# Where the moving rows and the joined rows begin in on-chip memory: start bytes of three operand tiles of a two-part transformer

## The chip, the cores and the metric

The kernel runs on one core of one Trainium2 chip. The metric is the device time of that core in microseconds, as the median of three runs. Four engines matter: TensorE (PE, its weight loads listed apart as PEld), VectorE (DVE), ScalarE (ACT) and, little used here, GpSimd (POOL). SyncE issues the weight transfers.

## What is computed

The reference takes x of 256 rows and 1024 columns through two blocks of two layers each, all in float32.

```python
# first block, layer l
h = rms_norm(x, g_mix[l]); proj = h @ w_in[l]
y_a, y_b, y_c, y_d = ...        # top-k attention, long convolution, short convolution, stick-breaking attention
merged = g0*y_a + g1*y_b + g2*y_c + g3*y_d
x = x + merged @ w_merge[l]
h2 = rms_norm(x, g_ffn[l]); gt = causal_dwconv(h2 @ w_ffn_gate[l], ffn_conv_w[l])
x = x + (silu(gt) * (h2 @ w_ffn_up[l])) @ w_ffn_down[l]
# second block, layer l
x = x + attention(rmsnorm(x, norm_mix[l])) @ w_out     # compressed attention in layer 0, dilated attention in layer 1
a, b = split(rmsnorm(x, norm_ffn[l]) @ w_up); x = x + (silu(a) * b) @ w_down
```

## The kernel before, in words

**The weights** come as a stream of 277 units of 1 MB (`weight_units`), each 1024 x 256, 256 x 1024 or 512 x 512. SyncE loads unit n into one of three slots of `raw`; ACT copies it, rounded, into one of four slots of `whi` (`make_high`, L439); DVE, for some units POOL, writes the remainder raw - whi into one of three slots of `wlo` (`make_low`, L447). A slot is used again when PE is through with the unit that was in it. Activations are split the same way into a high and a low half.

**Every large product** then consists of three matmuls for each pair of operand blocks (`three_passes`, L471 to L473): high by high, high by low, low by high. Each has a stationary block of 128 columns (512 bytes in each partition) that is loaded before the matmul, and a moving block of 256 columns (1024 bytes) or 512 columns (2048 bytes).

```python
nc.tensor.matmul(dst, left[0], right[0], start=first, stop=False)
nc.tensor.matmul(dst, left[0], right[1], start=False, stop=False)
return nc.tensor.matmul(dst, left[1], right[0], start=False, stop=last)
```

**The stages** run one after the other: a mixer or attention stage, an output product (`add_rows_product`), the up stage of the feed-forward (`ffn_up_stage`), its down product (again `add_rows_product`), and so on for four layers.

- `add_rows_product` (from L792) multiplies `joined` (the merged rows, or the context of an attention: 4 units, 96 matmuls) or `hidden` (the feed-forward's inner rows, `fT`: 11 units, 264 matmuls) with a weight unit. `joined` or `hidden` is stationary, the weights move, 512 columns at a time. At its end PE transposes the new x (L555), and ACT and DVE write the high and the low half of it, multiplied by the gain but not yet by the row's norm, to a tile of unscaled rows: `mixer_rows`, `ffn_rows`, `blocks_rows` or `dilated_rows`, after the stage that follows (`raw_T`, L542).
- A mixer or an up stage starts on these unscaled rows, so that PE need not wait for the norm. Unit 0 goes through `first_unit` (L656, L657, L665), then PE spreads the norm over the partitions (L597), then units 1 to 3 use the unscaled rows through `three_passes`. Meanwhile DVE and ACT write the scaled rows `hT`, and unit 4 and all later ones use `hT`. The weights are stationary here and the rows move, 256 columns at a time, but for units 4 to 11, 22 and 23 of a mixer and the first units of the attention stages, where the rows are stationary and the weights move.
- In an up stage (22 units, 48 matmuls each), DVE does for each pair of units the gate's part, the low half of the inner rows and two `make_low`, in an order written out by hand (`ffn_up_stage`, the vector engine's loop). Unit 5 needs the `make_low` that DVE does after the second pair's gate.

**Where tiles begin** is fixed by the order of allocation and, for tiles laid over a larger one, by a start in float32 elements (`over`, L269). The first tile, x, begins at byte 2176 of a partition. The starts that matter, modulo 512:

| tile | start given in the code | byte modulo 512 |
|---|---|---|
| `whi`, `wlo`, every slot | own tiles, 51840 and 84608 | 128 |
| `hT` | h_place (byte 10368) + 112 elements | 64 |
| `joined` | h_place + 96 elements | 0 |
| `hidden` | work (byte 120384) + 16 elements | 128 |
| `mixer_rows`, `ffn_rows` | work + 19072, + 14464 elements | 64 |
| `dilated_rows`, `query_rows`, `branch` | work + 17920, + 13824, + 4096 elements | 64 |
| `blocks_rows` | work + 15456 elements | 448 |

All blocks within a tile are multiples of 512 bytes apart, so an operand has its tile's start.

```python
hT_both = over("hT", at_h, LEAD_ROWS, [2, KT, S])                  # LEAD_ROWS = 512 // 4 - 16 = 112
joined_both = over("joined", at_h, LEAD_ROWS - 16, [2, KT, S])
for kind, rows_at in (("mixer", 19072), ("ffn", 14464), ("blocks", 15456), ("dilated", 17920)):
    raw_T[kind] = [over(f"{kind}_rows{i}", at_work, rows_at + i * KT * S, [KT, S]) for i in range(2)]
```

Of the kernel before, what the change touches and what calls it, by code (L numbers as in the profile page):

```python
# [30 lines left out]
S = 256  # L31
TT = S // P
KT = D // P
# [200 lines left out]
def two_part_transformer(nc, a, consts, onehots, out):  # L234
    ctx = ExitStack()
    with ctx:
# [11 lines left out]
        LEAD_ROWS = PHASE - 16  # L248
# [18 lines left out]
        at_h, at_work = place["h_place"], place["work"]  # L267

        def over(name, base, start, shape, dt=F32R):  # L269

            return nc.alloc_sbuf_tensor_at(name, [P] + shape, dt, offset=base + 4 * start)

        hT_both = over("hT", at_h, LEAD_ROWS, [2, KT, S])
        hT = [hT_both[:, i] for i in range(2)]
        joined_both = over("joined", at_h, LEAD_ROWS - 16, [2, KT, S])
        joined = [joined_both[:, i] for i in range(2)]

        ROWS = 32
# [261 lines left out]
            root_ready.close(n)  # L540

        raw_T = {}  # L542
        for kind, rows_at in (("mixer", 19072), ("ffn", 14464), ("blocks", 15456), ("dilated", 17920)):
            raw_T[kind] = [over(f"{kind}_rows{i}", at_work, rows_at + i * KT * S, [KT, S]) for i in range(2)]
        part_sum = stat[:, 152:156]
        root = stat[:, 4:4 + TT]
# [2266 lines left out]
```

How the kernel before makes its waits and increments, by code:

```python
        def begin(eng):  # L397
            if stage[0]:
                eng.wait_ge(stage_done.sem, COMPUTE * stage[0])
# [1 line left out]
        def end(eng):  # L401
            eng.drain().then_inc(stage_done.sem, 1)
# [10 lines left out]
        def v_wait(n):  # L413
            nc.vector.wait_ge(vector_step.sem, n)
# [9 lines left out]
        def s_wait(n):  # L424
            nc.scalar.wait_ge(scalar_step.sem, n)
# [6 lines left out]
        def make_high(act, upto):  # L432
            while stream.high < min(upto, len(stream.units)):
                n = stream.high
                act.wait_ge(raw_landed[n % RAW_SLOTS], 16 * (n // RAW_SLOTS + 1))
                if n >= HIGH_SLOTS:
                    act.wait_ge(*stream.freed[n - HIGH_SLOTS])
                act.activation(part(whi, n, HIGH_SLOTS), part(raw, n, RAW_SLOTS), ACT.Copy).then_inc(high_made, 1)
                stream.high += 1
# [1 line left out]
        def make_low(eng, n):  # L442
            eng.wait_ge(high_made, n + 1)
            if n >= LOW_SLOTS:
                eng.wait_ge(*stream.freed[n - LOW_SLOTS])
            eng.tensor_tensor(part(wlo, n, LOW_SLOTS), part(raw, n, RAW_SLOTS),
                              part(whi, n, HIGH_SLOTS).bitcast(F32), ALU.subtract).then_inc(stream.low[n][0], 1)
# [10 lines left out]
        def take_unit(pe, n):  # L459
            pe.wait_ge(*stream.low[n])
            _, kt, _, _ = stream.units[n]
            return [part(b, n, k).rearrange("p (k c) -> p k c", k=kt) for b, k in ((whi, HIGH_SLOTS), (wlo, LOW_SLOTS))]
# [18 lines left out]
        def await_pair(pe):  # L482
            if handed_over:
                pe.wait_ge(*handed_over.pop(0))
```

## Time and profile before

| | |
|---|---|
| median of 3 runs | 1798.43 us (1796.06 to 1802.86) |
| the profiled execution | 1797.66 us, of it 1795.9 us from the first to the last instruction |
| mean granted TensorE clock | 0.983 of full speed |
| PE | 1738.4 us busy, 13416 matmuls |
| DVE, ACT, POOL | 1226.3, 932.3, 125.0 us busy |
| memory traffic | 305.75 MB, mean 170 GB/s |

PE busy merges the times of matmuls that overlap, so a stage in which they follow each other without a gap counts as wholly busy, however far apart they start. What tells how fast PE works is the spacing: the time from the start of one matmul to the start of the next. A matmul's own duration (0.28 us at 256 columns, 0.39 us at 512) is over twice the spacing.

### The profile page before, as it was taken

How to read it: one execution, taken by the hardware profiler on the slowest of the kernel's cores; microseconds unless marked ns; L12 is line 12 of the kernel's file. 1: busy time of each engine (PE TensorE's matmuls, PEld its weight loads, DVE VectorE, ACT ScalarE, POOL GpSimd, SP SyncE). 2: the span in 40 equal slices, each digit the busy share in tenths (PEclk: the TensorE clock that was granted, in tenths of full speed). 3: DMA queues.
4: the chain of work that ended last, by engine and by line, in shares of the span. 5: the costliest groups of instructions: out<-in, count | busy, mean ns of one | idle time of the engine just before them, and what ended most of it. 6: DMA issues, size and time to landing. Idle time of an engine off the chain costs nothing.

```text
span 1795.9 us, 31735 instructions
## 1 busy us (share of the span) xinstructions
PE 1738.4 (97%) x13416; PEld 1641.0 (91%) x13416; DVE 1226.3 (68%) x1927; ACT 932.3 (52%) x1291; POOL 125.0 (7%) x35
## 2 busy tenths in 40 slices
PE   6999999999999999999999998889999999999998
PEld 6989999899989999999999898769998999889986
DVE  6994956797649868467887475977554656666553
ACT  5446655454445546654644356756443655655432
POOL 1620300000004503000000000000000000000000
PEclk9899999999999999999999989989999999999999
DMA  7684546556554554546465555415555486436551
GB/s 232 183 204 132 188 135 207 165 176 197 192 198 156 182 168 126 187 158 217 142 201 185 184 160 146 142 48 164 192 185 200 166 213 160 130 119 210 188 199 70
DMA packets 248636, 305.75 MB, mean 170 GB/s; under 512 B 9266, under 2 KB 223630, under 8 KB 248495
## 3 DMA queue, kind: packets, MB, share of 16 engines
q1 hardware_dynamic: 235959, 289.66, 49.3%
q10 hardware_dynamic: 12536, 14.06, 4.2%
q8 instruction: 106, 1.74, 0.4%
q14 instruction: 35, 0.29, 0.0%
HBM read 299.51 MB, written 4.19 MB: 169 GB/s over the span
## 4 chain that ended last, share of the span: by engine, by line
PE 76%; DVE 15%; ACT 4%; DMA 3%; issue 2%; DVEq 0%; ACTq 0%; SPq 0%
PE psum L471 23%; PE psum L472 22%; PE psum L473 22%; DVE wlo L447 3%; DVE psum L1482 3%; DMA raw<-in_w_in 1%; DVE work L1614 1%; PE psum L2483 1%; PE psum L2509 1%; DVE work L1612 1%; DMA raw<-in_a_w_in 1%; PE psum L2495 1%; ACT whi L439 1%; DMA raw<-in_b_w_q 1%; DVE work L1628 1%
## 5 line engine op out<-in xcount | busy, mean ns | idle before, releaser
L439 ACT ACTIVATE whi<-raw 128x2048 fp32r<-128x2048 f32 (+2 forms) x277 | 525.1, 1901 | 370.8 <-PE psum L473 261.3
L447 DVE TENSOR_TENSOR wlo<-raw,whi 128x2048 fp32r<-128x2048 f32 x249 | 566.8, 2281 | 198.0 <-PE psum L473 164.4
L471 PE MATMUL psum<-hT,whi 128*128 128x256 f32 x2160 | 608.2, 282 | 2.9 <-DVE wlo L447 1.5
L472 PE MATMUL psum<-hT,whi 128*128 128x256 f32 x2160 | 604.8, 280 | 0.0
L473 PE MATMUL psum<-hT,wlo 128*128 128x256 f32 x2160 | 604.7, 280 | 0.0
L471 PEld LDWEIGHTS psum<-hT,whi 128*128 128x128 f32 x2160 | 410.8, 190 | 4.2 <-DVE wlo L447 2.2
L472 PEld LDWEIGHTS psum<-hT,whi 128*128 128x128 f32 x2160 | 407.4, 189 | 0.2
L473 PEld LDWEIGHTS psum<-hT,wlo 128*128 128x128 f32 x2160 | 407.4, 189 | 0.0
L447 POOL TENSOR_TENSOR wlo<-raw,whi 128x2048 fp32r<-128x2048 f32 (+1 forms) x28 | 123.8, 4423 | 575.5 <-ACT whi L439 396.0
L471 PE MATMUL psum<-whi,hidden 128*128 128x512 f32 x352 | 137.2, 390 | 1.0 <-issue 1.0
L473 PE MATMUL psum<-whi,hidden 128*128 128x512 f32 x352 | 137.0, 389 | 0.0
L472 PE MATMUL psum<-wlo,hidden 128*128 128x512 f32 x352 | 137.0, 389 | 0.0
L1482 DVE SCALAR_TENSOR_TENSOR psum<-work,par,psum 128x256 f32<-128x256 f32 x240 | 94.6, 481 | 0.1
L471 PE MATMUL psum<-whi,hT 128*128 128x256 f32 (+1 forms) x320 | 92.4, 289 | 0.0
L472 PE MATMUL psum<-wlo,hT 128*128 128x256 f32 (+1 forms) x320 | 92.1, 288 | 0.0
L473 PE MATMUL psum<-whi,hT 128*128 128x256 f32 (+1 forms) x320 | 91.8, 287 | 0.0
L471 PEld LDWEIGHTS psum<-whi,hidden 128*128 128x128 f32 x352 | 66.1, 188 | 15.4 <-issue 1.7
L473 PEld LDWEIGHTS psum<-whi,hidden 128*128 128x128 f32 x352 | 66.1, 188 | 13.8
L472 PEld LDWEIGHTS psum<-wlo,hidden 128*128 128x128 f32 x352 | 66.1, 188 | 13.5
L910 ACT ACTIVATE work<-work 128x512 f32<-128x512 f32 x22 | 13.9, 633 | 118.6 <-DVEq L958 118.6
L1250 ACT ACTIVATE work<-psum 128x512 f32<-128x512 f32 (+1 forms) x40 | 23.2, 580 | 94.1 <-PE psum L473 94.0
L471 PE MATMUL psum<-branch,whi 128*128 128x256 f32 x256 | 71.3, 279 | 0.0
(367 smaller groups left out, 3073.1 us busy)
## 6 DMA issues: line engine op xcount, KB each, us to landing
raw<-in_w_in SPq DMA_DIRECT2D x78, 1024.0 KB, 5.5
raw<-in_ffn_w_up SPq DMA_DIRECT2D x44, 1024.0 KB, 5.0
raw<-in_w_ffn_gate SPq DMA_DIRECT2D x22, 1024.0 KB, 5.1
raw<-in_w_ffn_up SPq DMA_DIRECT2D x22, 1024.0 KB, 5.2
raw<-in_w_ffn_down SPq DMA_DIRECT2D x22, 1024.0 KB, 4.8
raw<-in_ffn_w_down SPq DMA_DIRECT2D x22, 1024.0 KB, 4.9
raw<-in_b_w_q SPq DMA_DIRECT2D x12, 1024.0 KB, 6.0
raw<-in_a_w_in SPq DMA_DIRECT2D x10, 1024.0 KB, 5.1
```

The costliest lines, as they stand in the source:

```text
L439: act.activation(part(whi, n, HIGH_SLOTS), part(raw, n, RAW_SLOTS), ACT.Copy).then_inc(high_made, 1)
L447: eng.tensor_tensor(part(wlo, n, LOW_SLOTS), part(raw, n, RAW_SLOTS), part(whi, n, HIGH_SLOTS).bitcast(F32), ALU.subtract).then_inc(stream ...
L471: nc.tensor.matmul(dst, left[0], right[0], start=first, stop=False)
L472: nc.tensor.matmul(dst, left[0], right[1], start=False, stop=False)
L473: return nc.tensor.matmul(dst, left[1], right[0], start=False, stop=last)
L1250: ins = act.activation(views[0], src[:, :, 0:views[0].shape[-1]], func)
L1482: ins = dve.scalar_tensor_tensor(acc, glu[:, ct, k:k + S], tap, acc, ALU.mult, ALU.add)
L1612: ins = dve.tensor_scalar(score[:, t, 0:L], rel[t][:, h, :], w, None, ALU.mult)
L1614: ins = dve.scalar_tensor_tensor(score[:, t, 0:L], rel[t][:, h, :], w, score[:, t, 0:L], ALU.mult, ALU.add)
L1628: n[t] = v_done(dve.match_replace(score[:, t, 0:L], top[:, t, :], score[:, t, 0:L], TAKEN))
L2483: mm = nc.tensor.matmul(slot(e)[:, st * keys:(st + 1) * keys], d_q[j // 2 % 2][lo:lo + DH, st, j % 2, t * P:(t + 1) * P], d_k[lo:lo + DH, ...
L2495: mm = nc.tensor.transpose(turn_bank(s, m)[:, i * P:(i + 1) * P], probs[:, 2 * (s % 2) + e, n * P:(n + 1) * P], ident)
```

## The change

`joined` begins at element 0 of its place in place of element 96, and the unscaled rows of the mixers and of the feed-forward stages 16 elements (64 bytes) later. By the table above, all three then begin at byte 128 modulo 512. No instruction is added, removed or moved in the program's order.

```diff
@@ -272,7 +272,7 @@
         hT_both = over("hT", at_h, LEAD_ROWS, [2, KT, S])
         hT = [hT_both[:, i] for i in range(2)]
-        joined_both = over("joined", at_h, LEAD_ROWS - 16, [2, KT, S])
+        joined_both = over("joined", at_h, 0, [2, KT, S])
         joined = [joined_both[:, i] for i in range(2)]
@@ -540,7 +540,7 @@
         raw_T = {}
-        for kind, rows_at in (("mixer", 19072), ("ffn", 14464), ("blocks", 15456), ("dilated", 17920)):
+        for kind, rows_at in (("mixer", 19088), ("ffn", 14480), ("blocks", 15456), ("dilated", 17920)):
             raw_T[kind] = [over(f"{kind}_rows{i}", at_work, rows_at + i * KT * S, [KT, S]) for i in range(2)]
```

## Rows read from the trace of the kernel before

**Rows 1.** The page: busy time of each engine, and its share of the chain.
```profile
PE 1738.4 (97%) x13416; PEld 1641.0 (91%) x13416; DVE 1226.3 (68%) x1927; ACT 932.3 (52%) x1291; POOL 125.0 (7%) x35
...
PE 76%; DVE 15%; ACT 4%; DMA 3%; issue 2%; DVEq 0%; ACTq 0%; SPq 0%
```
**Rows 2.** PE timeline (start us, us), first product of `joined`: first matmul, and what follows the last.
```profile
329.22 0.47 PE L471 MATMUL psum<-whi,joined 128*128 128x512 f32 x1 [0.26 <-issue]
...
351.60 0.60 PE L555 MATMUL psum<-cst,x 128*128 128x128 f32 x4
```
**Rows 3.** PE timeline, first product of `hidden`: first matmul, and what follows the last.
```profile
478.72 0.47 PE L471 MATMUL psum<-whi,hidden 128*128 128x512 f32 x1 [0.26 <-issue]
...
538.67 0.49 PE L555 MATMUL psum<-cst,x 128*128 128x128 f32 x3
```
**Rows 4.** PE timeline, first up stage: unit 1's second matmul, unit 4's first.
```profile
360.18 0.28 PE L472 MATMUL psum<-ffn_rows,whi 128*128 128x256 f32 x1
...
376.39 0.28 PE L471 MATMUL psum<-hT,whi 128*128 128x256 f32 x1
```
**Rows 5.** PE timeline, second up stage: the same two matmuls.
```profile
865.74 0.28 PE L472 MATMUL psum<-ffn_rows,whi 128*128 128x256 f32 x1
...
882.58 0.28 PE L471 MATMUL psum<-hT,whi 128*128 128x256 f32 x1
```
**Rows 6.** Windows, PE: window, its us, busy (matmuls), PEclk, DMA share, GB/s; rows moving.
```profile
354.30:359.30 5.00, 5.00 (x45) 1.00 0.01 3
549.00:563.00 14.00, 14.00 (x121) 1.00 0.36 100
...
1610.00:1624.00 14.00, 14.00 (x121) 1.00 0.49 156
```
**Rows 7.** The same view: `hT` moving, up stages 1, 2 and 4, then one mixer stretch.
```profile
384.00:476.00 92.00, 92.00 (x784) 1.00 0.61 204
884.00:984.00 100.00, 100.00 (x852) 1.00 0.60 198
...
1627.00:1711.00 84.00, 84.00 (x716) 1.00 0.59 197
791.40:834.30 42.90, 42.90 (x381) 1.00 0.55 196
```
**Rows 8.** The same view: before and after three changes of operands without a stop.
```profile
65.00:94.00 29.00, 29.00 (x249) 1.00 0.88 204
95.60:111.20 15.60, 15.60 (x140) 1.00 0.91 219
...
674.00:684.00 10.00, 10.00 (x91) 1.00 0.04 11
685.00:705.00 20.00, 20.00 (x172) 1.00 0.79 252
1061.00:1068.00 7.00, 7.00 (x64) 1.00 0.47 150
1069.00:1079.00 10.00, 10.00 (x88) 1.00 1.00 239
```
**Rows 9.** DVE timeline: the low half of unit 5, first three up stages.
```profile
379.74 2.29 DVE L447 TENSOR_TENSOR wlo<-raw,whi 128x2048 fp32r<-128x2048 f32 x1
...
885.57 2.29 DVE L447 TENSOR_TENSOR wlo<-raw,whi 128x2048 fp32r<-128x2048 f32 x1
...
1249.91 2.29 DVE L447 TENSOR_TENSOR wlo<-raw,whi 128x2048 fp32r<-128x2048 f32 x1
```
**Rows 10.** PE timeline: unit 5 begins, first stage (at 382.08) and second (888.23).
```profile
381.71 0.28 PE L473 MATMUL psum<-hT,wlo 128*128 128x256 f32 x1
382.08 0.39 PE L471 MATMUL psum<-hT,whi 128*128 128x256 f32 x1
382.31 0.28 PE L472 MATMUL psum<-hT,whi 128*128 128x256 f32 x1
...
888.23 0.28 PE L471 MATMUL psum<-hT,whi 128*128 128x256 f32 x1
```

## The prediction

> **What bounds the kernel now.** I read the page first. PE is busy 97% of the span, most slices show a 9, the granted clock is near full nearly everywhere, and the chain that ended last runs through PE for 76% [rows 1]. The change moves no instruction, so it can act only through how fast an engine reads or writes the moved tiles. PE is the engine to look at, and its busy time is of no use for this: overlapping matmuls count as busy whatever their spacing. So I went on to the timeline and took spacings, as the time between two starts over the number of matmuls between them. In the windows view a matmul counts when any part of it falls in the window, so there the spacing is (width + 0.28 us) / count.
>
> At 512 moving columns, `joined` takes 351.60 - 329.22 = 22.38 us for 96 matmuls, 233.1 ns each [rows 2]. `hidden` takes 538.67 - 478.72 = 59.95 us for 264, 227.1 ns each [rows 3]. Shape, line and moving tile are the same, both stages have a stall-free run, and what differs is the stationary tile's start: byte 0 modulo 512 for `joined`, 128 (that of the weights) for `hidden`. That is the best evidence that starts matter.
>
> At 256 columns there are two speeds. Units 1 to 3 of the first up stage: (376.39 - 360.18) / 143 = 113.4 ns [rows 4]. The same units of the second: (882.58 - 865.74) / 143 = 117.8 ns [rows 5]. Same tiles, same starts (rows at 64, weights at 128), other speed. So an unequal start doesn't set the speed but allows two, 4.4 ns apart. The slow one holds in units 1 to 3 of three up stages and of the second mixer and in unit 0 of the first up stage: 14.28 / 121 = 118.0 ns at 549, 117.0 and 118.0 at the last two up stages (one matmul of count is 1 ns there), 5.28 / 45 = 117.3 in unit 0 [rows 6]. `hT`, also at 64, runs at 92.28 / 784 = 117.7 ns through four up stages, yet at 43.18 / 381 = 113.3 ns in a mixer [rows 7]. A speed, once taken, lasts for hundreds of matmuls, until PE stops or the operands change.
>
> **The change part by part.** *`joined` to 128.* Afterwards it has exactly the starts of `hidden`, so I price it at its spacing: 4 products x 96 x (233.1 - 227.1) ns = 2.3 us, all on PE's path, since the stage before and after waits for it. Bounds: 0 if the difference had another cause, 2.3 if not.
>
> *The rows to 128.* No row shows 256 moving columns at equal starts. The bounds are 113.4 ns (the fast speed) and, on the bad side, half of the largest single spacing in the `joined` product, some 120.5 ns as an estimate (rows 2 give its mean, 116.5 per 256 columns, which is the nearer figure of that row). I take 113.4, because the only equal-start row, `hidden`, is 113.5 per 256 columns [rows 3] and keeps it through its whole run. Then:
> - Units 1 to 3 of up stages 3 and 4 and of mixer 2: 143 x 4.4 ns = 0.63 us each, 1.9 us. In up stage 3 the low half of unit 5 ends at 1249.91 + 2.29 = 1252.2 [rows 9], and PE gets to unit 5 only some 5 us later, so nothing takes it back; stage 4 is the same program.
> - Up stage 2: PE would be 0.63 us earlier, but DVE ends the low half of unit 5 at 885.57 + 2.29 = 887.86 [rows 9] and PE now begins it at 888.23 [rows 10]. Only 0.37 us of lead is there, and a stop costs a restart: the first spacing after one is 382.31 - 382.08 = 0.23 us instead of 0.12 in stage 1 (its first matmul lasts 0.39 instead of 0.28 us) [rows 10]. I keep 0.2 us. What is late next is DVE, which has the gate, the convolution and the low half in front of it.
> - Up stage 1: already fast in units 1 to 3, and it shows this stop: PE waits from 381.71 + 0.11 to 382.08, DVE having ended at 379.74 + 2.29 = 382.03 [rows 9, 10]. Only unit 0 gains, 47 x 4.4 ns = 0.2 us; DVE's chain begins with the norm behind unit 0 and moves with it.
>
> *Writes of the moved tiles* by ACT and DVE: same instructions, starts still multiples of 64 bytes. Nothing for them; `joined` is last written just before its product, so a dearer write would show there, and it would have to be 8 writes of each half, against which no row speaks and for which none does.
>
> Sum: 2.3 + 1.9 + 0.2 + 0.2 = 4.6 us. From the profiled execution's 1797.66 us that gives **1793.1 us**. The median of the runs is 0.8 us above that execution; the spread of the three, 6.8 us, is larger than the sum.
>
> **The large unknown: what `hT` does after the rows.** It runs 18 units of 48 matmuls in each up stage, 864 x 4.4 ns = 3.8 us if its speed flips. Today stages 2 to 4 go from slow rows to slow `hT` and stage 1 from fast to fast, until its stop, after which `hT` is slow (rows 4, 5 and 7 together). With the change the moving start goes from 128 to 64 at that point. Three changes of operands without a stop show a moving start going from 128 to 64: at 95.5 slow (29.28 / 249 = 117.6) turns fast (15.88 / 140 = 113.4), at 684 fast (10.28 / 91 = 113.0) turns slow (20.28 / 172 = 117.9), at 1068 fast (7.28 / 64 = 113.8) turns slow (10.28 / 88 = 116.8) [rows 8]. Each turned into the other. By that, fast rows hand a slow `hT`, as now, and the 3.8 us per stage stay where they are. I choose that.
>
> **The rivals.** *`hT` inherits the fast speed* where no stop follows, up stages 3 and 4: 2 x 3.8 = 7.7 us more, **1785.4 us**. For it: fast rows went to fast `hT` in stage 1, without a stop. Against: there the start did not change, and the three changes of [rows 8].
>
> *Only `joined` gains*: 256 columns settle in the slow speed at equal starts too, where stage 1 then loses what it has. **About 1795.4 us**, 1797.66 - 2.3.
>
> *Starts don't matter at all*, and `joined` is slow for another reason, such as its short run: **1797.7 us**. For it, two speeds at equal addresses; against it, two products that differ in one thing only. The Trainium skill, page "TensorE: Matmul & The Clock Gate", section "Step-by-step: what each phase is for", gives PE one read port for the moving operand and one for weight loads and says that loading the next weights takes no bandwidth from the running matmul; by it the change would be worth nothing, and this rival would be the forecast. The difference of rows 2 and 3 doesn't follow from it.
>
> *Equal starts collide at 256 columns.* The load of the next weights (512 bytes) and the moving rows (1024 bytes) begin at the same byte of the 512, and at 256 columns the next load begins as the last ends, which at 512 columns it doesn't. Place: the 6 x 192 = 1152 matmuls on moved rows, of which 4 x 143 + 47 are slow now, mean 115.8 ns. At 120.5 ns: 1152 x 4.7 ns = 5.4 us, less 2.3 for `joined`: **1800.8 us**. It decides against the change from 115.8 + 2.0 = 117.8 ns on, the present slow speed, and passes the 0.5% bound at about 126 ns. For it: no row of such a product. Against: `hidden`.
>
> **How the numbers follow.** Forecast 0.52; `hT` fast 0.18; only `joined` 0.12; nothing 0.06; collision 0.12. A measurement of this kernel can tell about 0.5%, 9 us, from no change, so faster means below 1789.4. The `hT` rival gives 0.17 of that; the forecast 0.07, where up stages 1 and 2 restart fast as well (2 x 3.8 us) or stops elsewhere fall on the fast side: faster 0.24. Slower: half the collision, and 0.03 for restarts that fall slow and for the clock, 0.09. Same 0.67. The range reaches down to the `hT` rival and up to the collision's price, 1785 to 1800.5; the forecast's own range is 1789 to 1797.
>
> **What would show it.** The `joined` product at about 227 ns and 21.8 us; units 1 to 3 of all up stages and mixer 2 at 113.4; `hT` behind them at 117.8 in stages 3 and 4, and a stop before unit 5 in stage 2. Rows at over 117.8 ns, or `joined` still at 233, would prove the sum wrong; `hT` at 113.3 over a whole up stage would prove the choice at the handover wrong.

## The result, and the profile after

The changed kernel takes 1786.88 us (median of 6 runs, 1785.55 to 1792.08) against 1798.51 us before (6 runs, 1796.06 to 1802.86): a ratio of 0.9939, 95% interval 0.9922 to 0.9956. That is 11.6 us less, inside the range of the prediction, but two and a half times the 4.6 us of its sum, and it came in another way: two large terms that the sum did not hold, of opposite sign, left a time within the range, which is in part luck. The profiled execution has a span of 1784.1 us, against 1795.9.

The page of the changed kernel, busy times and chain's engine:

```profile
PE 1725.9 (97%) x13416; PEld 1630.3 (91%) x13416; DVE 1226.8 (69%) x1927; ACT 931.5 (52%) x1291; POOL 125.1 (7%) x35
```

Against [rows 1] the counts are the same and DVE and ACT are as busy as before; PE is busy 12.5 us less, which is the whole gain. Nothing was hidden and nothing moved: the same matmuls follow each other more closely.

The PE timeline of the changed kernel (start us, us), in the order of [rows 2], [rows 4] and [rows 5]: the first `joined` product, then unit 1's second matmul and unit 4's first in up stages 1 and 2:

```profile
330.82 0.47 PE L471 MATMUL psum<-whi,joined 128*128 128x512 f32 x1 [0.27 <-issue]
...
352.69 0.38 PE L555 MATMUL psum<-cst,x 128*128 128x128 f32 x2
...
361.37 0.28 PE L472 MATMUL psum<-ffn_rows,whi 128*128 128x256 f32 x1
...
378.53 0.28 PE L471 MATMUL psum<-hT,whi 128*128 128x256 f32 x1
...
865.39 0.28 PE L472 MATMUL psum<-ffn_rows,whi 128*128 128x256 f32 x1
...
882.55 0.28 PE L471 MATMUL psum<-hT,whi 128*128 128x256 f32 x1
```

`joined` takes 21.87 us for 96 matmuls instead of 22.38: 0.51 us in each of four products, 2.0 us. The moved rows take (378.53 - 361.37) / 143 = 120.0 ns a matmul, and the same in stage 2, where 113.4 and 117.8 ns stood before. They became slower than either speed of before.

The windows of the changed kernel (window, its us, busy and matmuls, granted clock, DMA share, GB/s): first the rows in up stage 1, in the mixer and in up stage 4, as in [rows 6]; then `hT` moving in up stages 1, 2 and 4, as in [rows 7]; the third is like the fourth in both:

```profile
362.00:376.00 14.00, 14.00 (x119) 1.00 0.47 148
547.00:561.00 14.00, 14.00 (x119) 1.00 0.37 99
...
1600.00:1614.00 14.00, 14.00 (x119) 1.00 0.47 151
385.00:475.00 90.00, 90.00 (x797) 1.00 0.64 210
888.00:980.00 92.00, 92.00 (x814) 1.00 0.63 207
...
1624.00:1714.00 90.00, 90.00 (x797) 1.00 0.59 195
```

Rows: 14.28 / 119 = 120.0 ns in each. `hT`: 90.28 / 797 = 113.3 ns in all four up stages, against 117.7 in [rows 7]. So the gain is in `hT`, whose place did not change. How one passes to the other, up stage 1 (PE timeline; the first row is the last matmul on the rows):

```profile
378.41 0.28 PE L473 MATMUL psum<-ffn_rows,wlo 128*128 128x256 f32 x1
378.53 0.28 PE L471 MATMUL psum<-hT,whi 128*128 128x256 f32 x1
...
379.12 0.28 PE L473 MATMUL psum<-hT,wlo 128*128 128x256 f32 x1
...
476.36 0.28 PE L473 MATMUL psum<-hT,wlo 128*128 128x256 f32 x1
```

The first five spacings take 0.59 us, 118 ns each, and the 858 behind them (476.36 - 379.12) / 858 = 113.3 ns each, without a stop. At unit 5 there is none either: DVE ends its low half at 380.83 + 2.29 = 383.12, and PE, held up by the slower rows, comes only at 384.0.

```profile
380.83 2.29 DVE L447 TENSOR_TENSOR wlo<-raw,whi 128x2048 fp32r<-128x2048 f32 x1
```

**The sum by parts.** `joined` -2.0 us. `hT` in the up stages -15.4 us: in stage 1 from the first `hT` matmul to the first of the down product 476.89 - 378.53 = 98.36 us instead of 478.72 - 376.39 = 102.33, and 864 x 4.4 ns = 3.8 in each other. The rows +4.7 us, as an estimate: stage 1 17.16 - 16.21 = 0.95; stages 2 to 4 and mixer 2, 143 x 2.2 ns = 0.3 each; some 0.8 in mixer 1; 48 x 6 ns = 0.3 in each of the five units 0 that were fast. Together -12.7; the span shrank by 11.8, and the 0.9 us left are in the mixers and attentions, whose stretches change speed from execution to execution.

### The profile page after: what moved, and what is told of

It is laid out like the page before. It is cut to its first block, busy times and chain, and to the rows that moved or that the text cites. A ratio compares the mean times of both kernels' runs of the same rounds, so it can differ in the third digit from the quotient of the medians.

```text
span 1784.1 us, 31735 instructions
## 1 busy us (share of the span) xinstructions
PE 1725.9 (97%) x13416; PEld 1630.3 (91%) x13416; DVE 1226.8 (69%) x1927; ACT 931.5 (52%) x1291; POOL 125.1 (7%) x35
## 4 chain that ended last, share of the span: by engine, by line
PE 77%; DVE 14%; ACT 4%; DMA 4%; issue 2%; DVEq 0%; SPq 0%; ACTq 0%
PE psum L471 23%; PE psum L473 23%; PE psum L472 23%; DVE wlo L447 3%; DVE psum L1482 3%; DVE work L1614 1%; DMA raw<-in_w_in 1%; PE psum L2483 1%; ACT whi L439 1%; PE psum L2509 1%; DMA raw<-in_a_w_in 1%; PE psum L2495 1%; DMA raw<-in_b_w_q 1%; PE psum L656 1%; DVE work L1628 1%
```

## The experiments

The theory: **a moving block of 256 columns that begins where the weights do costs 120.0 ns. From 64 bytes before, two speeds are possible, 113.3 and 117.8 ns, and which one it is stays until PE stops or the operands change. What is handed over from a run at 120.0 ns is always the fast one.** The last sentence is put to the test below, and holds for less than it says. The rivals are named with each group of runs. "Draw" is short for a speed that neither the starts nor the instructions of a stretch fix; what does fix it was not found. Each run's profile is one execution; its times are of 4 to 10 runs, beside runs of the kernel before on the same chip.

### One part alone, and `hT` at equal starts

```diff
-        joined_both = over("joined", at_h, LEAD_ROWS - 16, [2, KT, S])
+        joined_both = over("joined", at_h, 0, [2, KT, S])
```


> Only joined at byte 128, all rows still at 64. Handover theory (the rows at 128 run at 120.0 ns and it is their handing over to hT that makes hT fast): joined products 226.7 ns a matmul, 2.3 us gained, units 1 to 3 of the up stages and hT behind them as before (117.8 ns in the four up stages), about 1796 us. Rival (the draw of hT's speed hangs on anything earlier, such as joined's own timing): hT fast in some up stages, each worth 3.8 us, 1781 to 1792 us.

```diff
-        ... ("mixer", 19072), ("ffn", 14464) ...
+        ... ("mixer", 19072), ("ffn", 14480) ...
```


> Only the feed-forward's unscaled rows at byte 128. Handover theory: 768 matmuls on these rows at 120.0 ns, some 2.9 us lost against the mean of before, and 863 matmuls on hT in each of four up stages at 113.3 ns, 15.3 us gained; no stop of PE before unit 5; sum about 1786 us. Rival (joined's start had a part in it): hT slow, 117.8 ns, in some or all of the four stages, 1790 to 1801 us.

```diff
-        ... ("mixer", 19072), ("ffn", 14464) ...
+        ... ("mixer", 19088), ("ffn", 14464) ...
```


> Only the mixers' unscaled rows at byte 128. Both theories: these 384 matmuls at 120.0 ns, 1 to 2 us lost, the matmuls on hT behind them not faster as a whole, since in a mixer the next units have hT stationary and stops for the transposes follow every few units; 1798 to 1801 us. Handover theory: the up stages as before. If the handover worked in the mixers too, the 47 matmuls of unit 4 would be at 113.3 ns in both.

On the changed kernel:
```diff
-        hT_both = over("hT", at_h, LEAD_ROWS, [2, KT, S])
+        hT_both = over("hT", at_h, 0, [2, KT, S])
```


> The changed kernel with hT at byte 128 as well. If equal starts of the weights and of a moving block of 256 columns cost 120.0 ns whatever comes before: all 6480 matmuls with hT moving at 120.0 ns. Of the changed kernel 5026 of them were at 113.3 and about 1400 at 117.8: 33 + 3 us lost, about 1822 us. Rival (120.0 ns belongs to the rows' place in the stage and not to their start): hT at 113.3 to 117.8 ns, 1780 to 1800 us.

| kernel | median us (runs) | ratio to before, 95% interval |
|---|---|---|
| `joined` alone | 1796.31 (10) | 0.9974, 0.9954 to 0.9994 |
| feed-forward rows alone | 1786.82 (4) | 0.9924, 0.9910 to 0.9939 |
| mixers' rows alone | 1801.36 (10) | 0.9995, 0.9977 to 1.0013 |
| all, and `hT` at 128 too | 1813.11 (4) | 1.0069, 1.0054 to 1.0084 |

The feed-forward's rows, 16 elements further on, carry the change: alone they give what the whole gives. `hT` in the four up stages, windows as above, of the kernel with the feed-forward's rows alone:

```profile
386.00:476.00 90.00, 90.00 (x797) 1.00 0.63 204
...
1627.00:1717.00 90.00, 90.00 (x797) 1.00 0.61 199
```

of the kernel with `joined` alone:

```profile
385.00:475.00 90.00, 90.00 (x796) 1.00 0.65 208
885.00:975.00 90.00, 90.00 (x766) 1.00 0.62 198
...
1628.00:1718.00 90.00, 90.00 (x767) 1.00 0.58 189
```

and of the kernel with the mixers' rows alone (its stage 2 is as slow as its stage 1):

```profile
386.00:476.00 90.00, 90.00 (x767) 1.00 0.62 197
...
1264.00:1354.00 90.00, 90.00 (x796) 1.00 0.61 201
1635.00:1725.00 90.00, 90.00 (x767) 1.00 0.58 188
```

797 matmuls in 90 us are 113.3 ns, 766 are 117.9. With the feed-forward's rows at 128, four of four are fast. With them at 64, one of four is fast, and not the same one: stage 1 in one kernel, behind its stop before unit 5, stage 3 in the other. Before the change none was. Neither kernel changed anything in these stages, so at unequal starts the speed of a stage is a draw. It is not an even one in every place: the 191 matmuls on `hT` at 283.68 us of the kernel before are slow in all seven kernels that have `hT` in one piece at 64 there. I had written for `joined` alone that the up stages would be as before; for stage 1 that missed, and the rival there, that any earlier timing plays a part, has this much right.

For the mixers' rows I had asked for one thing more: by the handover, unit 4, which has `hT` as the stationary side, should be fast in both mixers. It was in the first and not in the second, and the changed kernel does the same. There, without a stop behind rows at 120.0 ns (PE timeline of the changed kernel, mixer 1 and mixer 2; the last line is the first matmul of the next unit):

```profile
42.18 0.28 PE L472 MATMUL psum<-wlo,hT 128*128 128x256 f32 x1
...
47.39 0.28 PE L473 MATMUL psum<-whi,hT 128*128 128x256 f32 x1
...
562.70 0.28 PE L471 MATMUL psum<-whi,hT 128*128 128x256 f32 x1
...
568.36 0.19 PE L471 MATMUL psum<-whi,hT 128*128 128x68 f32 x1
```

That is (47.39 - 42.18) / 46 = 113.3 ns and (568.36 - 562.70) / 48 = 117.9 ns. So "always the fast one" fails where the operands change sides. Where the moving side alone passes from a costly start to 64 or 320 it holds in every trace: in all sixteen up stages of four kernels (the changed one, the feed-forward's rows alone, the two with `hT` at 320 and with stops, below), and for `branch` at 64 behind `hT` at 128 or 0, eight times in eight.

`hT` at 128 gives 752 in 90 us, 90.28 / 752 = 120.1 ns, in a stage where nothing else was touched: 120.0 ns belongs to the equal start, and not to the rows' part of the stage.

```profile
900.00:990.00 90.00, 90.00 (x752) 1.00 0.61 194
66.00:95.00 29.00, 29.00 (x244) 1.00 0.89 201
308.00:329.00 21.00, 21.00 (x188) 1.00 0.47 167
```

The second window has `hT` as the stationary side in mixer 1 and the weights moving: 29.28 / 244 = 120.0 ns, where `hT` at 64 gives 117.6 [rows 8]. So it is the two starts together that cost, and not a moving start of 128 by itself. The third is `branch`, at 64, behind `hT` at 128: 21.28 / 188 = 113.2 ns.

The time was forecast at 1822 us and is 1813. The up stages pay in full (3456 x 6.7 ns = 23 us). In the mixers the `branch` products were fast, and part of the slower matmuls may fall where PE would have waited for DVE, which no run took apart.

### A map of the starts

On the changed kernel, `joined` left at 128:
```diff
-  hT at h_place + 112, mixer_rows at 19088, ffn_rows at 14480
+  hT at h_place +  96, mixer_rows at 19056, ffn_rows at 14496
```


> A map of starts, joined at 128 throughout; the weights stay at 128. Here hT and the mixers' rows at 0, the feed-forward's rows at 192. Theory 'two speeds at any unequal start': these rows at 113.3 or 117.8 ns, hT at one of the two for a whole up stage as the draw falls, 1780 to 1796 us. Rival 'a start 128 bytes off collides' (joined at 0 took 233.1 ns at 512 columns): hT above 117.8 ns, over 1800 us.

```diff
+  hT at h_place +  16, mixer_rows at 19024, ffn_rows at 14528
```


> hT at 192, the mixers' rows at 384, the feed-forward's rows at 320. Theory of two speeds: 113.3 or 117.8 ns on all three, 1780 to 1796 us. Rival 'only a start after the weights' is free of the slow speed, since only starts before them were tried with rows moving': hT at 113.3 ns everywhere, about 1777 us.

```diff
+  hT at h_place +  80, mixer_rows at 18992, ffn_rows at 14560
```


> hT and the feed-forward's rows at 448, the mixers' rows at 256. Theory of two speeds: 113.3 or 117.8 ns on all three, 1780 to 1796 us. Rival 'distance decides': at 192 bytes from the weights no slow speed, hT at 113.3 ns in all four up stages and in the mixers, about 1772 us (rows fast too).

```diff
+  hT at h_place +  48, mixer_rows at 18976, ffn_rows at 14576
```


> hT at 320, the mixers' rows at 192, the feed-forward's rows at 0. Theory of two speeds: 113.3 or 117.8 ns on all three, 1780 to 1796 us. Rival 'distance decides': hT at 113.3 ns in all four up stages and the mixers, about 1772 us.

They took 1804.94, 1803.59, 1803.52 and 1784.85 us (ratios 1.0026, 1.0015, 1.0020 and 0.9917, the last with an interval of 0.9890 to 0.9945). In windows of the first: `hT` at 0, mixer rows at 0.

```profile
895.00:985.00 90.00, 90.00 (x761) 1.00 0.62 200
551.00:565.00 14.00, 14.00 (x119) 1.00 0.37 97
```

Of the second: `hT` at 192, mixer rows at 384, and, last, `hT` stationary in a mixer.

```profile
898.00:988.00 90.00, 90.00 (x766) 1.00 0.63 202
34.00:42.00 8.00, 8.00 (x69) 1.00 0.55 163
592.00:614.00 22.00, 22.00 (x197) 1.00 0.53 156
```

Of the fourth: the feed-forward's rows at 0, `hT` at 320 behind them, the rows again in stage 3, and `hT` in mixer 1.

```profile
362.00:376.00 14.00, 14.00 (x119) 1.00 0.44 142
889.00:979.00 90.00, 90.00 (x797) 1.00 0.66 210
1230.00:1245.00 15.00, 15.00 (x129) 1.00 0.50 161
181.00:201.00 20.00, 20.00 (x172) 1.00 0.75 234
```

The rows at 0 take 15.28 / 129 = 118.4 ns in stage 3, where stage 1 has 120.0. `hT` at 320 takes 20.28 / 172 = 117.9 ns in the mixer and 113.3 in the up stage.

| moving start modulo 512, weights at 128 | ns a matmul of 256 columns |
|---|---|
| 128, 384 | 120.0 |
| 0, 256 | 118.7 or 120.0 (both seen at 0) |
| 64, 320 | 113.3 or 117.8 |
| 192, 448 | 113.3 or 117.8, behind a stop nearly always 117.8 |

Starts 256 bytes apart behave alike, so what seems to count is the start modulo 256; the weights stood at 128 throughout. The last two rows differ: of the stretches of 40 or more matmuls with `hT` moving behind a stop, 110 of 197 were slow at 64 or 320, and 44 of 46 at 192 or 448 (PE timelines of ten kernels). Both rivals fell: a start further off (448) or one after the weights (192) is not better, since `hT` at 192 and 448 had the slow speed in all eight up stages, and in the fourth kernel `hT` was fast in the up stages but not throughout the mixers. The rival that a start 128 bytes off costs more than 117.8 ns held, for 0 and 256. I had expected two speeds there, and under 1796 us for the first three.

The fourth kernel supports the handover. Its rows are at 0, a costly start but another one, and `hT` at 320, which no kernel had tried: four of four up stages at 113.3 ns. That 320 is fast by itself, the rival here, is ruled out by the slow window in its mixer. And where `hT` is the stationary side and the weights move, a start at 192 or 448 was fast nearly throughout (22.28 / 197 = 113.1 ns), where 64 is mostly slow [rows 8].

### How few matmuls set the speed, and what a stop does

On the changed kernel the rows go back to 64 modulo 256, but for the last of their eight blocks:
```diff
+        class Halved:
+            def __init__(self, name, base, start):
+                self.body = over(name, base, start, [KT - 1, S])
+                self.tail = over(name + "_tail", base, start + (KT - 1) * S + 16, [1, S])
+            def __getitem__(self, at):
+                p, k, c = at
+                return self.tail[p, 0, c] if k == KT - 1 else self.body[p, k, c]
...
+            raw_T[kind] = [Halved(f"{kind}_rows{i}", at_work, rows_at - 64 + i * (KT * S + 64)) ...    # 19072, 14464
```


> The changed kernel with the mixers' and feed-forward's unscaled rows at byte 64 modulo 256 again, but for the last of their eight blocks of 256 columns, which alone begins at 128. Handover theory (a few matmuls at 120.0 ns are enough to set the fast speed for what follows): hT fast, 113.3 ns, in all four up stages, and the rows at 113.3 ns for most of the 21 matmuls behind each three slow ones, mean 114.5 to 115.5 instead of 120.0: 5 to 6 us less than the changed kernel, about 1781 us. Rival (the whole run of rows at 120.0 is needed, or what counts is that PE arrives late at unit 5): hT at 117.8 ns in at least two of the up stages, 1788 to 1796 us.

The same, and for `hT`:
```diff
+        hT = [Halved(f"hT{i}", at_h, 48 + i * (KT * S + 64)) for i in range(2)]
```


> The same, with the last block of hT at 128 as well (the rest of hT at 64 modulo 256). Handover theory: every group of 24 matmuls has three at about 120 ns and some transition, the rest at 113.3 whatever the stops did: mean about 115 ns for hT moving. Against the kernel of the run before this one, the up stages lose some 3456 x 1.5 ns = 5 us, and the mixers and attentions gain on the 1400 matmuls that are slow now, 1400 x 2.8 ns = 4 us: about the same, 1778 to 1785 us. Rival (the fast speed after a few matmuls is not kept): mean above 116.5 ns, over 1790 us.

On the changed kernel, in the up stage's PE loop:
```diff
                     w = take_unit(pe, n0 + n)
+                    if n in (6, 14):
+                        pe.drain()
```


> The changed kernel, with PE drained ahead of units 6 and 14 of each up stage. A stop costs at most 0.5 us, 8 of them 2 to 4 us. Theory (a stop draws the speed anew, the handover's gain lasts until then): hT fast in units 4 and 5 of each up stage, then fast or slow for stretches of 8 units (384 matmuls, 1.7 us each), some of the 8 slow: 1788 to 1800 us. Rival (hT's speed belongs to the addresses now in use, stops or not): all stretches at 113.3 ns, 1788 to 1791 us.

`hT` in the up stages in one piece as in the first of these, in halves as in the second in the mixers and the compressed attention:


> The kernel with the last block of the rows at 128 (median 1779.97 us), with hT in one piece at 64 in the up stages, and with its last block at 128 in the mixers and in the compressed attention alone. Theory: the up stages keep 113.3 ns, in the mixers hT moving goes from a mix of 113.3 and 117.8 to a mean of about 115, and branch behind it is fast; against the run with the last block at 128 everywhere 3456 x 1.0 = 3 to 5 us less, about 1777 us. Rival (the kept state is lost at every stop for the transposes, so that the slow matmuls cost as much as they save there): 1780 us or more.

| kernel | median us (runs) | ratio to before, 95% interval |
|---|---|---|
| last block of the rows | 1779.97 (4) | 0.9898, 0.9862 to 0.9935 |
| last block of rows and `hT` | 1781.44 (4) | 0.9911, 0.9879 to 0.9942 |
| two stops in each up stage | 1797.16 (10) | 0.9988, 0.9971 to 1.0005 |
| last block of the rows, and of `hT` in the mixers | 1782.28 (6) | 0.9904, 0.9879 to 0.9928 |

**The stops** gave back most of the gain, 10.3 us by medians of different sessions, 9 by the two ratios. Each costs some 0.4 us (in stage 1, 392.24 to 392.84 us for what takes 0.23 otherwise), 3 us in all; three slow stretches of 382 matmuls are 5 us. The profiled execution is 14.5 us longer than that of the changed kernel: 8.2 us in the four up stages, as this sum says, and 6.4 in the mixers and attentions, where nothing was changed. Windows of that kernel, the two stretches behind the stops in stages 1, 2 and 3:

```profile
394.00:436.00 42.00, 42.00 (x359) 1.00 0.65 206
440.00:482.00 42.00, 42.00 (x359) 1.00 0.61 200
904.00:944.00 40.00, 40.00 (x342) 1.00 0.66 207
950.00:990.00 40.00, 40.00 (x356) 1.00 0.62 210
1272.00:1312.00 40.00, 40.00 (x356) 1.00 0.58 190
1317.00:1357.00 40.00, 40.00 (x355) 1.00 0.56 185
```

Units 4 and 5 ahead of the first stop were fast in all four stages. Behind it: slow, slow, slow, fast, fast, fast (42.28 / 359 = 117.8, 40.28 / 342 = 117.8, 40.28 / 356 = 113.1), and fast twice in stage 4. Same instructions, same addresses: behind a stop the speed is a draw again.

**Three matmuls** in 24 are enough for the rest. One turn of the loop in the kernel with the rows' last block at 128, PE timeline:

```profile
363.34 0.28 PE L480 MATMUL psum<-ffn_rows_tail,whi 128*128 128x256 f32 x1
363.46 0.27 PE L481 MATMUL psum<-ffn_rows_tail,whi 128*128 128x256 f32 x1
363.57 0.28 PE L482 MATMUL psum<-ffn_rows_tail,wlo 128*128 128x256 f32 x1
363.69 0.28 PE L480 MATMUL psum<-ffn_rows,whi 128*128 128x256 f32 x1
```

The spacings around the tail are 0.11 to 0.12 us, and then 0.113 on average until the next tail. Its windows, the rows in stage 1 and `hT` in stages 2 and 4:

```profile
362.00:376.00 14.00, 14.00 (x125) 1.00 0.47 151
890.00:980.00 90.00, 90.00 (x797) 1.00 0.64 210
1625.00:1715.00 90.00, 90.00 (x796) 1.00 0.61 199
```

The rows take 14.28 / 125 = 114.2 ns instead of 120.0, and `hT` is fast in all four stages. 1152 x 5.8 ns would be 6.7 us, and the medians are 6.9 us apart. That agreement is loose: the medians are of different sessions, the intervals of the two ratios overlap, and the profiled execution, the slowest of the four, is 2.6 us shorter in the up stages and 3.8 longer in the rest. By its median the kernel is the fastest of the study. In stages 1 and 2 the stop before unit 5 is back, and the draw with it: in this profile it fell fast twice, in that of the last kernel it fell slow in stage 1:

```profile
384.00:474.00 90.00, 90.00 (x766) 1.00 0.63 205
```

With `hT`'s last block at 128 too, the up stages run at 90.28 / 791 = 114.1 ns with no draw left in them, and the mixers' `branch` products were fast; what that gains it pays in the up stages. The last kernel was to have both, 1777 us, and took 1782.28 us, the time of its rival. The rival's reason does not hold, though. Windows of it, `hT` moving behind a stop and then `hT` stationary, in the mixers:

```profile
287.00:307.00 20.00, 20.00 (x177) 1.00 0.60 214
580.00:609.00 29.00, 29.00 (x247) 1.00 0.61 182
```

With `hT` moving the expected mean came, 20.28 / 177 = 114.6 ns, stops or not. With `hT` stationary the block at 128 costs and hands nothing on: 29.28 / 247 = 118.5 ns, above both speeds of before. That and the slow stage 1 cost time; how the 5 us split was not measured. The medians of the three, 1780.0 to 1782.3 us, are nearer to each other than their intervals are wide.

## Why the prediction was right and wrong

- **`joined` to 128: right.** 2.3 us forecast, 2.0 us in the profile. Alone it measures 0.26%, 0.06 to 0.46%, which is 4.7 us and holds 2.3; draws of the up stages, one of them fast in the profile, are in that number too.
- **The rows to 128: wrong, and with the wrong sign.** "I take 113.4, because the only equal-start row, `hidden`, is 113.5 per 256 columns." They take 120.0. The step that failed is the carrying over from 512 columns to 256. The load of the next 128 stationary columns runs beside the matmul. How long it takes is seen where the moving block is too short to cover it: with 68 columns, in the index unit of the second mixer, two matmuls that are 24 apart start 2.68 us apart (PE timeline of the kernel before):

```profile
569.60 0.27 PE L472 MATMUL psum<-wlo,hT 128*128 128x68 f32 x1
...
572.28 0.28 PE L472 MATMUL psum<-wlo,hT 128*128 128x68 f32 x1
```

  So a load and what belongs to it would take 111.7 ns, if the load is what sets this spacing. At 512 columns that is half of a spacing of 227 ns, and a load held up by a few nanoseconds is not seen; at 256 it is all of it. `hidden` would then show only that the moving stream is not disturbed. That this is why the equal start costs 6.7 ns at 256 columns and nothing at 512 is argued, not shown, and it does not cover `joined`, which paid 6 ns at 512 columns, where a load has as much room as in `hidden`. The rival of the collision had the place and nearly the price: I had put 120.5 ns.
- **The handover: wrong.** "Fast rows hand a slow `hT`" rested on three changes of operands, all from one of the two speeds into the other, and in all three the operands changed sides, so that the stationary start moved as well. The rows were in neither speed and kept their side, so the rule had nothing to say of them. It is no rule for its own case either: at 96.03 us of the changed kernel slow hands over slow (97 to 112 us, 130 matmuls, 15.28 / 130 = 117.5 ns). The rival that `hT` is fast had stages 3 and 4; it was all four, since stages 1 and 2, for which I had a stop by DVE before unit 5, lost it to the slower rows. A part that got slower took a wait away, and with it the draw that the wait brings.
- **The time**: 1785.4 us was given to the rival with 0.18, and the time came within 1.5 us of it. That is luck: the rival had two stages at 3.8 us and rows that gain, and what came was four stages and rows that lose. The collision (0.12) and the fast `hT` had been priced as exclusive; they happened together, +4.7 and -15.4 us, and the first brought the second: the feed-forward's rows alone make all four stages fast.
- **Starts don't matter: wrong.** The runs show 113.3 to 120.0 ns for one instruction, with nothing changed but starts. By the Trainium skill (page "TensorE: Matmul & The Clock Gate", "Step-by-step: what each phase is for") loading the next weights takes no read bandwidth from the running matmul. A forecast of no change from it fails; whether the sentence itself does depends on which of the two is held up, and what speaks against it is `joined`, 233.1 ns at 0 and 227.8 at 128 with 512 moving columns.
- **The scatter.** The kernel before spreads over 1790.45 to 1807.25 us in 19 runs, the kernel with the feed-forward's rows alone over 1785.92 to 1790.53 in 4, the changed one over 1785.55 to 1792.08 in 6. Four draws of 3.8 us would span 15 us, which is near that of the kernel before; that the runs' times differ for this reason was not measured run by run.

**Left open:** what in the memory or in PE makes 256 bytes the period, why a costly moving start is followed by the fast speed, why that fails for the stationary side, and what the draw hangs on. The weights were never moved from 128, so that the two starts count only relative to each other is shown from one side only.

## What to carry to other kernels

Where PE is busy all the time, busy shares hide the spacing: divide a stretch by its matmuls, by operand and start address, before looking for anything else. With both operands at the same start, a moving block of 256 float32 columns took 6% longer here, and at unequal starts the speed may be a draw that lasts until the next stop: here a few matmuls on a moving block at the costly start just ahead of a long run on the same side, and no stop within it, settled it. A figure taken at one block width does not carry over to another at which a second stream becomes as long as the first.

## What the runs showed of the hardware that had not been expected

- A matmul of 256 float32 columns, stationary 128 columns, with nothing else changed: 113.3, 117.8, 118.7 or 120.0 ns by the starts of the two operands, and at all starts tried but 128 and 384 (against 128) by history too.
- The state outlives the change of tile, of weight slot and of accumulator bank (858 spacings in a row) and ends at a stop of under half a microsecond.
- At 512 moving columns the cost of the stationary operand's start is 6 ns a matmul (`joined` at 0 against 128), with no draw: in each of the four products at 0, 22.4 us, in each at 128, 21.9 us.
